# A mixture-of-experts ring: gate, up and down weights of a slot refilled together after the old expert's last product

## The reference

```python
def swiglu(x, w_gate, w_up, w_down):
    return (jax.nn.silu(x @ w_gate) * (x @ w_up)) @ w_down

def moe(u, router_w, router_bias, exp_w_gate, exp_w_up, exp_w_down, ...):
    ...                                  # eidx: 8 experts of each token, gw: their gates
    yb = lax.map(expert_block, (xb, block_e)).reshape(NB * MOE_BLOCK, D) * buf_w[:, None]
    routed = jnp.zeros_like(u_pad).at[buf_t].add(yb)[:T]
    return routed + swiglu(u, sh_w_gate, sh_w_up, sh_w_down)
```

## Time and profile before

| | us |
|---|---|
| median of 3 runs | 2801.4 |
| lowest, highest | 2800.69, 2803.92 |
| profiled execution | 2804.71 |
| its span, first to last instruction | 2802.9 |
| TensorE busy in the span | 2630.9 (94%) |
| VectorE, ScalarE, GpSimd busy | 1270.0, 732.4, 800.1 |
| mean granted TensorE clock | 0.965 |

### The profile page before, as it was taken

One profiled execution on the slowest core, in us unless ns is written; L12 is line 12 of the kernel. 1 busy time (PEld: TensorE's weight loads), 2 busy tenths in 40 slices (PEclk: granted clock), 3 DMA queues, 4 the chain that ended last, 5 costly groups with the idle time before them and its releaser, 6 DMA issues. The chain is left out here.

```text
span 2802.9 us, 37288 instructions
## 1 busy us (share of the span) xinstructions
PE 2630.9 (94%) x12050; PEld 1459.5 (52%) x12051; DVE 1270.0 (45%) x1949; ACT 732.4 (26%) x1209; POOL 800.1 (29%) x922
## 2 busy tenths in 40 slices
PE   7997999998989899999999978999999989999993
PEld 3564888874667556666666646633333323333332
DVE  3333333333747487853111166354444444444446
ACT  3213333333424300001100031223333223332322
POOL 1000221211534100000000002456656555556545
PEclk8998999998999999999999989999999999999995
DMA  6530000011011111210210511389888998998944
GB/s 247 216 117 23 19 16 16 23 46 49 24 43 33 32 34 34 64 45 25 96 45 4 206 38 70 120 309 318 261 257 261 331 345 252 313 312 282 344 113 187
DMA packets 161015, 390.32 MB, mean 139 GB/s; under 512 B 20819, under 2 KB 107935, under 8 KB 133001
## 3 DMA queue, kind: packets, MB, share of 16 engines
q1 hardware_dynamic: 132689, 319.65, 31.4%
q0 software_dynamic: 28224, 69.29, 10.4%
HBM read 337.68 MB, written 70.45 MB: 146 GB/s over the span
## 5 line engine op out<-in xcount | busy, mean ns | idle before, releaser
L2580 PE MATMUL ps<-big 128*64 x1344 | 597.7, 598 | 0.0
L2524 POOL DMA_INDIRECT big<-u_rows,big x336 | 365.8, 1089 | 148.7 <-issue 76.9
L2580 PEld LDWEIGHTS ps<-big 128*64 128x64 f32 x1344 | 177.8, 137 | 351.8 <-issue 351.8
L1760 PE MATMUL ps<-big 128*128 128x352 f32 x1152 | 346.8, 461 | 5.7 <-SPq L1696 5.7
L2595 PE MATMUL ps<-big 128*64 x672 | 303.9, 595 | 2.1 <-DVE big L2737 2.1
L1760 PEld LDWEIGHTS ps<-big 128*128 128x128 f32 x1152 | 219.7, 191 | 129.1 <-SPq L1696 6.1
L849 PE MATMUL ps<-big 128*128 128x352 f32 x576 | 205.5, 463 | 2.0 <-DMA big<-in_w_in 1.9
L1304 PE MATMUL ps<-big 128*128 128x352 f32 x576 | 185.2, 469 | 10.2 <-DVE big L1524 7.6
L2595 PEld LDWEIGHTS ps<-big 128*64 128x64 f32 x672 | 92.3, 138 | 194.0 <-issue 194.0
L1774 PE MATMUL ps<-big 128*128 128x352 f32 x576 | 174.4, 459 | 1.6 <-DVE big L1894 1.6
L2540 POOL DMA_INDIRECT y_rows<-big x84 | 145.9, 1736 | 103.5 <-issue 89.4
(11 more groups left out here) (580 smaller groups left out, 4242.4 us busy)
## 6 DMA issues: line engine op xcount, KB each, us to landing
big<-in_exp_w_gate SPq DMA_DIRECT2D x64, 1024.0 KB
big<-in_exp_w_up SPq DMA_DIRECT2D x64, 1024.0 KB
big<-in_exp_w_down SPq DMA_DIRECT2D x64, 1024.0 KB
big<-in_ada_w SPq DMA_DIRECT2D x24, 1024.0 KB, 8.1
big<-in_w_in SPq DMA_DIRECT2D x48, 512.0 KB, 4.1
y_rows<-pick SPq DMA_DIRECT2D x16, 512.0 KB, 14.2
big<-y_rows SPq DMA_DIRECT2D x16, 512.0 KB, 10.7
big<-in_w_in SPq DMA_DIRECT2D x6, 1024.0 KB, 5.3
```

Source lines behind the costliest of these rows:

```text
L1760: ins = pe.matmul(ps[:, c, 0:CW], ring_g[:, q % 2, j, :], k.hT[:, j, c * CW:(c + 1) * CW], start=(j == 0), stop=(j == KT - 1))
L2524: g.indirect_dma_start(out=x_rows[:, u, x * 256:(x + 1) * 256], out_offset=None, in_=u_quarters, in_offset=bass.IndirectOffsetOnAxis(idx_i ...
L2580: pe.matmul(ps[0:SUB, 2 + u, :].rearrange("p (g f) -> p g f", f=FF), xT[:, u, j, 0:SUB], gate_up[:, j], start=(j == 0), stop=(j == KT - 1))
```

## The change

`reload` no longer waits for `up_done`, and issues no part ahead of the others. It waits for expert e-1 to have landed, counts `weights_ready` up, waits for `down_done` of the old expert's last block, and issues gate, up and down one after the other.

```diff
             def reload(e, s, blocks_before, loads_before):
-                wait_before_addressed(sp, up_done, blocks_before, sp_passed)
-                load_part(k, sp, e, s, 0)
-                load_part(k, sp, e, s, 1)
                 sp.wait_ge(weights_loaded[(s - 1) % NW], loads_before * 48)
                 sp.sem_inc(weights_ready, 1)
                 wait_before_addressed(sp, down_done, blocks_before, sp_passed)
-                load_part(k, sp, e, s, 2)
+                for part in range(3):
+                    load_part(k, sp, e, s, part)
```

## The result

The changed kernel takes **2878.8 us** (median of 4 runs, 2875.6 to 2886.2), the kernel before 2802.0 on the same chip: a ratio of 1.0277, with a 95% interval of 1.0256 to 1.0298. The forecast was 2865 in a range of 2836 to 2896. Its profiled execution took 2879.7 us, 75.0 more than that of the kernel before.

What follows compares the result with a forecast made beforehand. TensorE sets the expert stage's pace at 10.82 us per block while weights arrive in time. Late loads 72.0 less 16.5 lost today give +55.5, clock +8: 63.5 on 2804.7 is 2868, median 2865 us, range 2836 to 2896.

Steps and rivals of the forecast that it cites:

- tight places: Blocks 6, 35 to 41, 52, 53, 70 to 74, 79, where a load's slack is short; 16 of 60 cases.
- L: Time from a load's first issue to readiness; taken as 13.0 us behind products, 12.5 behind the landing before.
- five firsts: First blocks of the tight groups, 6, 35, 52, 70 and 79, each forecast 5.9 us late.
- Rival 2: Weight loads: a queue holding one expert alone lands all three parts in under 8.6 us; not slower, 2793 us; chance 0.03.
- a: First block of a tight group, its load waiting for the old expert's products: 5.9 us late.
- c: Third in a tight group, its load again waiting for products, two blocks after the first: 4.0 us late.
- b: Next expert in a tight group, its load waiting for the landing of the one before: 1.9 us late.
- block 41: Needs two loads more than block 40, experts 31 and 32, one behind the other: 14.6 us.
- clock: TensorE at half speed for 4 to 6 us behind pauses of 3.9 us or longer: +8 us in all.
- Top rate: Weight loads: three parts back to back run at 413 GB/s, L 9 us; about +6, 2807 us; chance 0.05.
- One batch per block anyway: Runs of one-block experts: only the order shifts, only the first of each group pays; +24, 2825 us; chance 0.07.
- Adds first each time: Weight loads: the queue dries up and row adds get in first, L 16.7 us; 2900 us with clock; chance 0.08.

Runs made afterwards that it cites:

- the queue alone: Changed against the kernel before: landing of the expert ahead awaited before gate and up, which still leave after the up products; 2836.3 us, ratio 1.0125.
- the late issue alone: Changed against the kernel before: gate and up wait for the down products, the landing wait stays just before the down part; 2918.6 us, ratio 1.0413.

## Why the prediction held, and where it was off

**The tight places: right.** The late blocks are 6, 12, 35 to 41, 52, 53, 70 to 74 and 79, and the blocks right behind some of them. No gather or row add ends a pause of TensorE there: all 14 end with the hidden rows, and in the chain a weight load stands behind them.

**L: right as a sum, wrong in its make-up.** 13.0 was taken, and 12.5 to 13.6 measured at the five firsts. But the prediction let the row adds stand at the head of the load, as in the earlier trace rows. In the changed kernel they meet its end: by the table of issues the up part lands 3.3 us after the gate part (7.9 + 0.4 - 5.0), the down part 4.6 after the up part (12.0 + 0.5 - 7.9). The DMA queues in the last 3 us of the load for block 35, 2198 to 2201 us (packets, MB, share of the 16 engines; software_dynamic is GpSimd's queue, hardware_dynamic that of the loads):

```profile
q0 software_dynamic: 183, 0.52, 82.1%
q1 hardware_dynamic: 29, 0.11, 10.4%
```

At a head the adds cost about as much (a down part alone took 8.2 and 7.4 us at blocks 6 and 52 of the kernel before, and 4.8 and 4.9 in the run of that kernel with the add first, where the adds were through before it), so the sum did not notice. It is also why two parts cost so little: they are nearly through when the adds come (in the run with the up part alone moved, GpSimd's queue carries nothing from 2381 to 2387 us, and the load for block 52 has landed at 2387.9). Rival 2 drew on the same fact, that one part alone took 7 to 8 us for 2.5 us of data. Its reason, the next expert's parts in the queue, isn't what the runs show: the 4.9 us at block 52 were reached with the next gate part 1.2 us behind in the queue. And L without any row add is still 10.0, above its 8.6.

Two readings behind L and the late issue were not right. Expert 3, the nearest row for 12.5 us, was not alone in the queue, since the gate part of expert 4 left 2.6 us behind its own, at 1827.41; in the changed kernel it is alone and takes 12.4 (1825.73 to 1838.1), so the figure stood. And gate and up leave 9.6 us later in a run of one-block experts by the prediction's own rows (2188.53 to 2198.11), not 10.8; the sum does not use it.

**Term by term**, in us of lateness, worked out from the starts of the blocks' first products:

| term | forecast | measured |
|---|---|---|
| a: blocks 6, 35, 52, 70, 79 | 5 x 5.9 = 29.5 | 6.5, 5.7, 5.9, 6.0, 6.8 = 31.0 |
| c: blocks 37, 39, 72, 74 | 4 x 4.0 = 16.0 | 6.1, 6.0, 5.8, 3.4 = 21.3 |
| b by a load: 53, 71, 73 | 3 x 1.9 = 5.7 | 3.6, 3.6, 3.2 = 10.5 |
| b: 36, 38, 40 | 3 x 1.9 = 5.7 | 0, not late by loads |
| block 41 | 14.6 | 10.8 |
| block 12 | 0.5 | 2.3 |
| loads together | 72.0 | 75.8 |
| clock: 7, 13, 36, 38, 40, 42, 75, 80 | 8 | 15.5 |
| less what was lost before | -16.5 | -16.5 |
| difference | 63.5 | 74.8 |

That the loads together come to 75.8 against 72.0 is in part luck, since the terms are off both ways.

**The step that failed is the clock,** 15.5 us where 8 was taken and 13 was the upper bound. Stretches behind three pauses (length, busy of each engine, TensorE clock, DMA share, GB/s), to be read beside the earlier trace rows:

```profile
1873.10:1879.30 6.20, 0.01 (x2) 0.01 (x1) 1.43 (x3) 2.76 (x4) 0.18 (x1) 0.78 0.78 255
1879.30:1883.40 4.10, 4.10 (x12) 1.31 (x14) 3.40 (x5) 0.38 (x1) 2.02 (x2) 0.50 1.00 422
...
2227.60:2233.40 5.80, 0.03 (x1) 0.03 (x1) 1.45 (x3) 2.76 (x4) 0.18 (x1) 0.84 0.73 250
2233.40:2238.40 5.00, 5.00 (x14) 1.57 (x16) 3.38 (x5) 0.38 (x1) 2.24 (x3) 0.50 1.02 429
...
2744.80:2751.30 6.50, 0.00 (x1) 0.01 (x1) 1.42 (x3) 2.76 (x4) 1.21 (x3) 0.67 0.60 160
2751.30:2757.20 5.90, 5.90 (x16) 1.88 (x18) 3.50 (x5) 1.44 (x2) 3.12 (x3) 0.50 1.05 417
```

Behind each, the clock is at 0.50 (1.2 GHz) for 4.1 to 5.9 us, as foreseen, and its products take 0.85 us apart instead of 0.43 (1881.03 in the chain above). Block 80 starts 13.44 us behind block 79 (2751.99, 2765.43), 2.6 late with its weights there long before. Wrong was the hiding: "the next block waits 1.9 us for its load anyway". It held at 53, 71 and 73, where the slow step before is covered by the wait. At 36, 38 and 40 the load was there 5.5 to 6.9 us before the block, more than the 3.9 needed, and the step was 1.4 to 2.6 too long for the clock alone. The steps before 36 and 40 (columns as above):

```profile
2204.90:2217.00 12.10, 12.10 (x51) 3.81 (x50) 4.81 (x8) 2.77 (x5) 6.51 (x7) 0.88 0.70 234
2263.20:2277.00 13.80, 13.80 (x51) 4.34 (x52) 5.36 (x8) 2.89 (x4) 6.39 (x7) 0.78 0.91 338
```

TensorE waits for nothing in them, and the missing clock, 12% of 12.1 us and 22% of 13.8, is 1.5 and 3.0 us for steps that are 1.4 and 2.6 too long. And a slow step also ends its down products later, so that the next load starts later: the loads of experts 27, 29, 56 and 58, behind the c terms, left 12.2 to 13.0 us after a block's start instead of 10.6. That is the main reason why three of the four c came out at 6 and not at 4. The prediction had the clock as an addition; in a loop where products release loads and loads release products it enters the load's account, too. That the clock makes these steps long is read from busy time and granted clock; no run took it away.

**12.5 for loads behind a landing was one value for two.** In blocks 36 to 41, where TensorE stands a quarter of the time, it was 10.4 to 11.0 for four loads and 13.0 for the fifth (expert 31); at 53, 71 and 73, 14.0 to 14.4. Why, no run shows. The two errors (41 too dear, 53 to 73 too cheap) nearly cancel.

**The rivals.** Top rate (L = 9): no, 12.5 to 13.6; even without row adds 10.0. By the Trainium skill ("DMA: Bandwidth & Descriptors", section "Anatomy of one DMA — SWDGE (gpsimd) path"), whose figures are for transfers that GpSimd issues while these are SyncE's, 2.0 us and 3.15 MB over 436 GB/s are an estimate of 9.2 us. The measured 10.0 without row adds, with gathers only in its last 2 us, comes near, 12.5 to 13.6 with both doesn't. One batch per block anyway: no, runs go on losing. Adds first each time (L = 16.7): no.

**What stays open.** How the rest of the 77 us divides between the late issue and the empty queue. The five firsts, 31 us, are the late issue; the queue alone costs 35, in other places; but the two meet in the runs, and the late issue alone was isolated only at blocks 6 and 35, since in its run a signal was held back as well. A form that issues all three parts behind the products without emptying the queue and without holding the signal (with a second engine that counts the landings, for instance) wasn't tried.

## What to carry to other kernels

In a ring of buffers, what counts is the time from the release of a slot to the readiness of the new content, against the number of steps until it is needed: find the tightest cases by walking the schedule, since an average of DMA load (here 68% to 103%) says nothing about them. Loading in pieces, each as early as its old content is dead, and without waiting for the load ahead to land, was worth 77 us here. And where one engine's list both signals readiness and waits for release, look at each signal that stands behind each wait: a count of `weights_ready` held back behind a release made blocks 5 us late whose weights had landed.

## What the runs showed of the hardware

Row adds are dear for what they move: the stretch at 156 GB/s with all DMA engines busy, and 3 us of a 13 us load of 3 MB that vanish without them. Behind pauses of TensorE of 5.4 to 6.5 us the clock was at half for 4 to 6 us of work, and the next step took 1.4 to 2.6 us longer where no wait covered it, while the steps behind the lates of about 1 us of the kernel before took 10.82 us.
